# Moving matmul blocks of TensorE ahead of two sets of output transposes in a two-block mixer kernel

## The reference, cut to what matters

```python
h = modulate(rmsnorm(x, norm1_g), shift, scale)
u = split(h @ w_in)              # widths by IN_SPLITS, u[7] is z, u[10] the merge's gates
y_m = mlstm_mixer(u[0], u[1], u[2], u[3], ...)    # ends in rmsnorm per head, times sigmoid(o)
y_a = attention_mixer(u[4], u[5], u[6], ...)      # differential attention, ends in a head norm
y_s = ssd_mixer(u[7], u[8], u[9], ...)            # scan, times silu(z), ends in a group norm

def gated_merge(y_m, y_a, y_s, gate_pre, w_m, w_a, w_s, w_o):
    g_m, g_a, g_s = jnp.split(jax.nn.sigmoid(gate_pre), N_BRANCH, axis=-1)
    return (g_m * (y_m @ w_m) + g_a * (y_a @ w_a) + g_s * (y_s @ w_s)) @ w_o

x = x + mod[2][:, None] * gated_merge(y_m, y_a, y_s, u[10], ...)
```

## Time and profile before

| | us |
|---|---|
| median of 3 runs | 4592.31 |
| lowest and highest | 4591.52, 4597.65 |
| profiled execution | 4591.14 |
| its span in the trace | 4589.4 |
| PE busy in the span | 3806.1 |
| DVE busy | 3121.8 |
| POOL busy | 1260.6 |
| ACT busy | 734.2 |

### The profile page before, as it was taken

One profiled execution on the slowest core, in us unless ns is written; L12 is line 12 of the kernel. 1 busy time (PEld: TensorE's weight loads), 2 busy tenths in 40 slices (PEclk: granted clock), 3 DMA queues, 4 the chain that ended last, 5 costly groups with the idle time before them and its releaser, 6 DMA issues.

```text
span 4589.4 us, 42544 instructions
## 1 busy us (share of the span) xinstructions
PE 3806.1 (83%) x13554; PEld 2117.5 (46%) x13554; DVE 3121.8 (68%) x6439; ACT 734.2 (16%) x1805; POOL 1260.6 (27%) x1220
## 2 busy tenths in 40 slices
PE   7879879998889898888788887787789878777776
PEld 3334437643467776676654542232233246322222
DVE  3756537677567677664668758878876746788666
ACT  1231110024312221212100110010110021101000
POOL 0001100001033343331034333343354500335433
PEclk9889989999879999899899999999999999999999
DMA  5423226534200000004199999999999931899998
GB/s 209 174 101 146 75 92 229 211 147 158 106 5 24 5 24 8 24 5 168 65 390 413 367 361 421 399 402 412 395 415 404 422 151 74 351 410 398 421 421 354
DMA packets 140144, 1073.77 MB, mean 234 GB/s; under 512 B 15504, under 2 KB 15888, under 8 KB 21520
## 3 DMA queue, kind: packets, MB, share of 16 engines
q0 software_dynamic: 112608, 820.04, 44.0%
q1 hardware_dynamic: 27312, 251.02, 14.4%
HBM read 1060.51 MB, written 10.49 MB: 233 GB/s over the span
## 4 chain that ended last, share of the span: by engine, by line
PE 40%; DVE 36%; DMA 10%; issue 7%; POOL 3%; ACT 2%; DVEq 1%; SPq 0%; POOLq 0%; ACTq 0%
PE bank L199 19%; DVE arena L2901 11%; DMA arena<-in_uv,arena 7%; PE bank L2855 4%; DVE arena L2908 4%; POOL arena L2885 3%; PE bank L2415 3%; PE bank L2138 2%; DVE arena L442 2%; DVE arena L221 2%; ACT arena L211 2%; PE bank L2130 2%; DVE arena L217 2%; DVE arena L560 2%; PE bank L1616 2%
## 5 line engine op out<-in xcount | busy, mean ns | idle before, releaser
L2855 PE MATMUL bank<-arena 128*128 128x512 f32 x3072 | 1507.6, 621 | 402.8 <-DVE arena L2908 396.9
L199 PE MATMUL bank<-arena 128*128 128x128 f32 (+5 forms) x4896 | 1304.1, 426 | 76.8 <-DVE arena L217 18.2
L2885 POOL DMA_INDIRECT arena<-in_uv,arena x768 | 832.5, 1084 | 1309.2 <-PE bank L2855 628.9
L2855 PEld LDWEIGHTS bank<-arena 128*128 128x128 f32 x3072 | 541.2, 192 | 1342.5 <-DVE arena L2908 837.1
L2901 DVE CUSTOM_DVE_ANT_0 arena<-arena 128x1024 f32<-128x1024 f32 x768 | 941.6, 1226 | 279.8 <-DMA arena<-in_uv,arena 204.7
L199 PEld LDWEIGHTS bank<-arena 128*128 128x128 f32 (+3 forms) x4896 | 816.1, 196 | 554.8 <-issue 425.6
L211 ACT ACTIVATE arena<-arena 128x1 f32<-128x1 f32 (+6 forms) x1089 | 331.7, 305 | 2620.2 <-DVE arena L2901 1821.8
L211 ACT ACTIVATE arena<-bank 128x512 f32<-128x512 f32 (+3 forms) x464 | 248.3, 535 | 1090.4 <-PE bank L2117 500.9
L2908 DVE TENSOR_SCALAR arena<-arena 128x128 f32<-128x128 f32 x768 | 287.8, 375 | 173.4 <-ACT arena L211 112.9
L2200 POOL TENSOR_TENSOR arena<-arena 128x512 f32<-128x512 f32 x128 | 163.5, 1277 | 449.5 <-PE bank L2130 442.2
L442 DVE CUSTOM_DVE_ANT_0 arena<-arena 128x1024 f32<-128x1024 f32 x192 | 240.5, 1253 | 33.7 <-DMA arena<-in_w_rows 22.0
(11 more groups left out here) (251 smaller groups left out, 2854.4 us busy)
## 6 DMA issues: line engine op xcount, KB each, us to landing
arena<-in_w_rows SPq DMA_DIRECT2D x50, 1024.0 KB, 5.0
arena<-in_w_in SPq DMA_DIRECT2D x16, 2048.0 KB, 7.8
arena<-in_wq SPq DMA_DIRECT2D x14, 2048.0 KB, 8.7
arena<-in_dn_w SPq DMA_DIRECT2D x12, 2048.0 KB, 9.2
arena<-in_w_up SPq DMA_DIRECT2D x11, 2048.0 KB, 8.8
arena<-in_dn_wo SPq DMA_DIRECT2D x8, 2048.0 KB, 11.1
arena<-in_w_rows POOLq DMA_DIRECT2D x14, 1024.0 KB, 5.5
arena<-in_uv,arena POOLq DMA_INDIRECT x768, 10.5
```

Of the source, the lines that this page charges most:

```text
L199: t = p.e.matmul(out, l, r, start=(i == 0), stop=(i == n - 1))
L2855: t = p.e.matmul(by[half], m["dg"][ee % 4], m["uv"][r][:, 1024 + 512 * half:1536 + 512 * half], start=(ee == 0), stop=(ee == 127))
L2885: g.e.indirect_dma_start(out=m["uv"][q % 7], out_offset=None, in_=self.I["uv"], in_offset=bass.IndirectOffsetOnAxis(ap=m["idx"][n % 2][:, ...
```

## The change

z's projection becomes a function of its own and PE runs it between the mLSTM heads and the mLSTM out transposes; in `pe_sproj` the two steps of the gates' generator that went with its tiles are run first. The branches of the merge are taken in the order 0, 2, 1 (m, s, a) on SP, PE, ACT and DVE, and PE runs the first two of the first half between the attention heads and the attention's out transposes. `pe_merge` does the remaining four. No other engine's program changes but for the branch order.

```diff
+    def pe_sz(self, p):
+        ch = self.ring.use(p, 8, 512)
+        run(self.pe_tokens(p, "sp.z", ch, self.hT, (2, 3), 512, lambda i: self.A.of("sp.z", i)))
+        self.ring.done(self.P.of("sp.z", 3))
+
     def pe_sproj(self, p, m, Gm):
         side = self.pe_sgates(p, m, Gm)
-        ch = self.ring.use(p, 8, 512)
-        for _ in self.pe_tokens(p, "sp.z", ch, hT, (2, 3), 512, lambda i: A.of("sp.z", i)):
+        for _ in range(2):
             next(side, None)
-        self.ring.done(P.of("sp.z", 3))
...
+    BRANCHES = (0, 2, 1)
+
     def sp_merge(self, s, m):
         for half in range(2):
-            for br in range(3):
+            for br in self.BRANCHES:
                 self.ring.load(s, self.I["w_branch"][br * 2 + half], 4, 512)
...
+    def pe_branch(self, p, yT, half, br):
+        ch = self.ring.use(p, 4, 512)
+        for i in range(2):
+            k_ = (half, br, i)
+            b = self.banks.take(p, "mr.b", *k_)
+            mm(p, b, [(yT[:, 4 * br + k, 128 * i:128 * i + 128], ch[:, k, :]) for k in range(4)]
+               ).then_inc(*self.P.up("mr.b", *k_))
+            self.banks.give(("mr.b", *k_), self.V.of("mr.m", *k_))
+        self.ring.done(self.P.of("mr.b", half, br, 1))
+
     def pe_merge(self, p, m, yT):
         for half in range(2):
-            for br in range(3):
-                ch = self.ring.use(p, 4, 512)
...
+            for br in self.BRANCHES:
+                if half or br == 1:
+                    self.pe_branch(p, yT, half, br)
         self.pe_bcast(p, "mr", m["wide"])
         for i in range(2):
-            p.wait_ge(*V.of("mr.sum", 1, 2, i))
+            p.wait_ge(*V.of("mr.sum", 1, 1, i))
...
         weave_lag([self.pe_mhead(p, m, n) for n in range(8)])
+        self.pe_sz(p)
         self.pe_mout(p, m)
...
         weave_lag([self.pe_dhead(p, L["d"], n) for n in range(8)])
+        for br in self.BRANCHES[0:2]:
+            self.pe_branch(p, self.yT, 0, br)
         self.pe_dout(p, L["d"])
```

## The result

| | before | changed |
|---|---|---|
| median of 12 runs each, us | 4592.71 | 4604.54 |
| lowest and highest | 4588.99, 4604.56 | 4593.21, 4615.51 |
| profiled execution | 4591.14 | 4601.46 |
| its span | 4589.4 | 4599.7 |

The changed kernel is slower: the ratio of the times is 1.0030, with a 95% interval of 1.0021 to 1.0038. The medians differ by 11.8 us and the two profiled spans by 10.3 us, against 10.7 us forecast. The interval reaches from 9.6 to 17.5 us slower, so the runs don't tell 10.7 from 11.8.

What follows compares the result with a forecast made beforehand. It took a chain shared by PE and DVE to bound the kernel, with a gate chain on ACT and DVE close beside PE's. Part A +9.5 and part B +1.2 gave +10.7 us, 4603.0 us with the median's 1.2, range 4594 to 4610.

Steps and rivals of the forecast that it cites:

- z as a block: PE after mLSTM's heads: z's two tiles take 15.65 us at a low start, 13.93 at a high one.
- The stage's end: mLSTM's output: out transposes and DVE wait for z, so the stage ends 9.7 us later, at 261.1.
- The gate chain: Crow, Silu, softplus, decay and sums on ACT and DVE: 21.4 us from mLSTM's stage end, so sums' transposes +7.5 us.
- p1's low start: SSD's channel tile p1 starts at the low clock after PE's wait for the sums: +2.0 us, between nothing and 2.2.
- The merge: After the attention's output: PE waits 5 us for a bank, last matmul at 649.6 against 648.4: +1.2 us (-0.9 to +3.6).
- The order m, s, a: Merge branches: the new order alone moves no work and costs nothing.
- faster, PE's saved work counts: Rival at the wait for running sums after p0: 6 us won there, 5.3 in the merge, 4581 us; chance 0.05.
- Same: Rival: the delay is there but every unknown falls low, +4.8 us, 4597 us; chance 0.29.
- Faster, by the clock: Rival: filled gaps remove both low starts of PE (1.7 + 2.2 us), nothing else moves, 4588.4 us; chance 0.03.
- Slower still: Rival in the merge: half 1's loads share the engines with the gates' fetch, gates 5 us later, 4608 us; chance 0.10.

Runs made afterwards that it cites:

- part B alone: Kernel before with only branches m and s ahead of the attention's out transposes, order m, s, a; z unmoved: +0.7 us against before, interval 0.9994 to 1.0011.
- a_gates: Kernel before with z ahead of mLSTM's out transposes and ACT's softplus and decay before the Silus of crow and z; merge unchanged: -1.9 us against before.
- after_gates: The whole change plus ACT's softplus and decay ahead of the Silus of crow and z: -1.9 us against before, interval 0.9985 to 1.0002.
- all_one: Kernel before with z split around mLSTM's first out transposes, ACT's softplus and decay first, only branch m ahead of attention's out transposes: -13.5 us, ratio 0.9973.
- a_split: Kernel before with z's first tile ahead of mLSTM's first out transposes, its second between the two sets; ACT's order unchanged: +4.2 us, interval 0.9996 to 1.0018.
- all_split: Kernel before with z split, ACT's softplus and decay first, m ahead of and s between the attention's out transposes: -12.7 us against before, ratio 0.9974.
- all_best: all_split with the gates' fetch cut into six DMAs: -8.3 us against before, interval 0.9976 to 0.9997.

## Why the prediction was right

The sign, the size (+10.7 forecast, +11.8 measured, +10.3 in the profiled spans) and the steps held. That the size is met to about 1 us is in part luck, since the interval is 8 us wide, and two terms (p1's start and the merge) were off by 0.6 and 0.9 us in opposite directions:

- *z as a block.* Forecast 15.65 us with a low start; in the changed kernel it took 17.80 - 2.1 = 15.7 us.
- *The stage's end.* Forecast 9.7 us later; 23.9 - 14.3 = 9.5.
- *The gate chain.* Forecast 21.4 us from the stage's end; 281.25 - 259.63 = 21.6. The sums' transposes were forecast 7.5 us later and came 45.5 - 37.9 = 7.6 us later. PE's wait before them: 11 forecast, 9.9 measured, since p0 took 9.83 us at its low start and not 8.7; as PE had to wait, this cost nothing.
- *p1's low start.* Forecast 2.0, at most 2.2. It was 9.65 - 7.06 = 2.6: this bound was too narrow, since it was taken from the two starts that the earlier trace rows show, and others are dearer. With it the shift at p4's convolution was 10.5 us (77.7 against 67.1) instead of 9.5.
- *The merge.* Forecast +1.2 from a wait of 5 us for one bank; the wait was 4.94 us, and the term +0.3, because the branches ran at the full clock without the 0.6 us that I had added, and the stage ended 7.9 us later instead of 8.9. In the run of part B alone, with a low start, the term was +2.2. Both lie within -0.9 to +3.6.
- *The order m, s, a.* Priced at nothing. It was in every run of part B and never alone, so this stays argued.

Of the rivals, "faster, PE's saved work counts" named the right place and the right condition: the sums have to be ready when p0 ends. With ACT's order changed it was nearly met (PE waits 0.84 us for them in a_gates, 1.46 in after_gates), but its sum, 11 us faster, was far too large: after_gates can't be told from before. The 6 us that it counted from p0's earlier start became 1.4 us in a_gates, because p0 began at the low clock (9.88 us instead of 6.97) behind the stage's late end, and the bank in the merge did not come in time. all_one is 13.5 us faster, but with z and the branches placed otherwise. "Same" is excluded by the interval, though closely: its lower end is 9.6 us, and the prediction drew the line at 9.2. "Faster, by the clock" (by the Trainium skill, TensorE: Matmul & The Clock Gate, HAM oscillation — how this bites in real kernels) did not come: z ran mostly at 2.4 GHz, but PE still stood for 5.87 us between the two sets of transposes, and p0 behind them began low (2.9 us lost, in the shadow of the wait); and a new gap came behind p0, with a loss of 2.6 us at its end. The trace agrees with the rule as far as PE's own speed goes; the rule says nothing of the engine that waits for what was pushed back. "Slower still" had its mechanism half right: loads behind the gates' fetch do meet it, but the fetch kept its time (10.0 us in the changed kernel against 10.2) and the loads behind it grew from 5.0 to 11.8. Nothing was added to DVE's path.

Between p4 and the attention heads' end all_one gives back 1.8 us, but all_split gives back 1.2 and all_best 0.1 with the same program up to there, so this is within the scatter of single executions. What stays open is where a_split loses 3 us in that stretch, and the 1.5 us between the change's 11.8 and its span's 10.3; the changed kernel's runs spread over 22 us, and one profile can't say.

## What to carry to other kernels

If PE stands idle in front of a transpose and another engine waits for that transpose, work put into the gap is free only up to the length of the gap, so cut the work to the gaps (here 7 us into 5.5 us) rather than moving the block whole. Before PE's work is moved out of a stage, look at the chains that start at that stage's beginning on other engines; when PE's part shrinks they can become the bound, and here 9.0 us of the 21.6 of that chain was work that could go behind. In a merge whose loads are issued on one queue, count what is behind each wait: in part B alone the gates were there at 625.0 us, the next weights at 627.5 and the bank at 628.9, so removing one wait bought nothing.

## What was not expected

Starts of PE from the low clock cost between 1.7 and 2.9 us for the same kind of matmul. The same tile in the same place, z's first in the kernels that leave it there, took 8.68 us in one profile and 9.82 in another, against 6.97 at the full clock. So the price of one start is known only to about a microsecond.

Six DMAs of 512 KB in place of one of 3 MB held SP's queue for 4.21 us instead of 0.33, and the first of them was with ACT only some 4.4 us after its issue (its median time to land is 7.4 us for 512 KB, against 10.2 for the whole). The loads issued behind a large fetch landed after it (11.9 us instead of 5.0), while the fetch was not slowed by them (10.1 us against 10.2).
